# Second attention of a two-block transformer kernel: split queries and keys through memory, one 192-column score product for two short ones

## What is computed

```python
DILATED_BRANCHES = ((128, 1), (512, 4), (2048, 16))
def dilated_attention(q, k, v, rel_bias):
    for window, dil in DILATED_BRANCHES:
        o, l = dilated_window_branch(q, k, v, rel_bias, window, dil)
        ...
    w = jax.nn.softmax(jnp.stack(lses, axis=0), axis=0)
    return jnp.einsum('ibsh,ibshd->bshd', w.astype(q.dtype), jnp.stack(outs, axis=0))
...
q, k, v, zu, zv = jnp.split(z, ...)          # z = rms_norm_2(x) @ w_in, 8 heads of 64
attn = dilated_attention(q * 64 ** -0.5, k, v, rel_bias)
mix = jnp.concatenate([attn, sgu], axis=-1) @ w_out
```

## Time and profile before

| | |
|---|---|
| Times of 3 runs | 2572.89, 2575.97, 2576.0 us |
| Median | 2575.97 us |
| Span of the profiled execution (first to last instruction) | 2570.8 us |
| Busy: PE, weight loads, DVE, ACT, POOL | 2539.0, 2118.1, 1558.9, 1063.0, 1254.9 us |
| Granted PE clock | 0.998 of full speed |
| DMA | 372.39 MB, 41.8% of the 16 engines' span |

### The profile page before, as it was taken

One profiled execution on the slowest core, in us unless ns is written; L12 is line 12 of the kernel. 1 busy time (PEld: TensorE's weight loads), 2 busy tenths in 40 slices (PEclk: granted clock), 3 DMA queues, 4 the chain that ended last, 5 costly groups with the idle time before them and its releaser, 6 DMA issues. The chain is left out here.

```text
span 2570.8 us, 35208 instructions
## 1 busy us (share of the span) xinstructions
PE 2539.0 (99%) x12974; PEld 2118.1 (82%) x12974; DVE 1558.9 (61%) x2581; ACT 1063.0 (41%) x2107; POOL 1254.9 (49%) x1003
## 2 busy tenths in 40 slices
PE   8999999999999999999999999999999999999998
PEld 7888888777888888888888878998889888888886
DVE  6455444685437545444698751168656666587787
ACT  5332333684224332322444541169745323254443
POOL 4587675354526656555231774548545444200204
PEclk9999999999999999999999999999999999999999
DMA  6565655706551222221752345423143333364434
GB/s 218 203 237 207 237 218 193 266 18 202 192 180 66 82 82 88 77 82 66 294 185 96 117 154 189 106 67 85 51 134 116 115 106 117 136 232 146 173 105 157
DMA packets 162710, 372.39 MB, mean 145 GB/s; under 512 B 21538, under 2 KB 42658, under 8 KB 158882
## 3 DMA queue, kind: packets, MB, share of 16 engines
q1 hardware_dynamic: 162540, 370.15, 41.8%
HBM read 268.01 MB, written 101.83 MB: 144 GB/s over the span
## 5 line engine op out<-in xcount | busy, mean ns | idle before, releaser
L2421 POOL TENSOR_TENSOR WL<-WRAW,WH 128x512 fp32r<-128x512 f32 (+1 forms) x150 | 249.9, 1668 | 298.6 <-ACT WH L1101 298.6
L856 PE MATMUL PS<-HH,WL 128*128 128x512 f32 (+1 forms) x976 | 367.2, 376 | 1.1 <-DVE HS L2022 1.1
L859 PE MATMUL PS<-HH,WH 128*128 128x512 f32 (+1 forms) x976 | 366.1, 375 | 0.0
L858 PE MATMUL PS<-HL,WH 128*128 128x512 f32 (+1 forms) x976 | 366.1, 375 | 0.0
L1658 DVE TENSOR_TENSOR WL<-TS,WH 128x512 fp32r<-128x512 f32 x228 | 225.6, 994 | 169.7 <-ACT WH L1101 169.6
L920 PE MATMUL PS<-WH,DAL 128*128 128x512 f32 x756 | 294.4, 389 | 0.1
L921 PE MATMUL PS<-WL,DAH 128*128 128x512 f32 x756 | 294.1, 389 | 0.0
L922 PE MATMUL PS<-WH,DAH 128*128 128x512 f32 x756 | 294.1, 389 | 0.0
L2612 POOL TENSOR_TENSOR X<-X,DV 128x512 f32<-128x512 f32 x56 | 89.7, 1628 | 353.4 <-DVE DV L2085 270.8
L1101 ACT ACTIVATE WH<-TS 128x512 fp32r<-128x512 f32 x228 | 138.4, 621 | 179.8 <-POOL TS L2437 179.6
L856 PEld LDWEIGHTS PS<-HH,WL 128*128 128x128 f32 x976 | 183.7, 188 | 34.2 <-DVE HS L2022 1.3
(11 more groups left out here) (422 smaller groups left out, 6052.9 us busy)
## 6 DMA issues: line engine op xcount, KB each, us to landing
WRAW<-in_u_f SPq DMA_DIRECT2D x56, 512.0 KB, 3.8
WRAW<-in_u_in SPq DMA_DIRECT2D x54, 512.0 KB, 4.1
WRAW<-scr_t SPq DMA_DIRECT2D x52, 512.0 KB, 3.7
scr_h<-HS SPq DMA_DIRECT2D x96, 256.0 KB, 2.0
WRAW<-in_u_gu SPq DMA_DIRECT2D x44, 512.0 KB, 3.4
scr_t<-TTa SPq DMA_DIRECT2D x19, 1024.0 KB, 4.8
WRAW<-in_u_out SPq DMA_DIRECT2D x24, 512.0 KB, 3.6
scr_x<-X SPq DMA_DIRECT2D x24, 512.0 KB, 4.9
```

The costliest lines, as they stand in the source:

```text
L856: e.matmul(PS[:, b, 0:wd], wl[:, blk(kk)], op_moving(q, kk, c0, wd, 0), start=(kk == 0), stop=False)
L858: e.matmul(PS[:, b, 0:wd], wh[:, blk(kk)], op_moving(q, kk, c0, wd, 1), start=False, stop=False)
L859: mm = e.matmul(PS[:, b, 0:wd], wh[:, blk(kk)], op_moving(q, kk, c0, wd, 0), start=False, stop=(kk == 3))
L2421: e.tensor_tensor(lo, raw, hi.bitcast(F32), ALU.subtract).then_inc(*c.inc("w_lo_p", i))
```

## The change

1. The projection takes q and k tiles in turn (q of two heads, k of the same two), by another order of the weight's columns. Each tile is now split when it is drained: ACT writes the high part QKH, DVE the low part QKL from the same PSUM bank. Keys are laid out in groups of 192 columns, 128 strided ones and a copy of 64 near ones.
2. SP stores both parts to memory (32 DMAs, 10.5 MB) and loads each head back with the parts in the rows PE wants: two DMAs for the keys (64x1536), four for the queries (64x1024), 1.8 MB a head (14.7 MB in all). Heads 0 and 1 are loaded before the attention, head h + 2 after the last scores of head h, ahead of its bias table.
3. PE's four short score products of a step become two of 192 columns.
4. ACT's `keys_hi`, `queries_hi` and POOL's `keys_lo`, `queries_lo` are gone. `spread` goes from ACT to POOL, with two ARB buffers.
5. Head 0's keys no longer sit in a weight slot, so one more weight unit of the output projection is split before the attention (N_EARLY 3).

```diff
-            pairs = [(qs[:, blk(i % 4)], key_hi(h)[:, :]), (qs[:, blk(i % 4)], key_lo(h))]
-            w.wait_ge(*c.at("k_dn", (h, 1, 2)))
-            w.wait_ge(*c.at("q_dn", s // 4))
+            kk, col = K2[h % 2], 512 * hf + 128 * r
+            w.wait_ge(*c.at(f"hd_{h % 2}", h))
+            q2 = [q[:, col:col + 128] for q in Q2[h % 2]]
...
-                e.matmul(PS[:, b, 0:128], q_, keys(k_, 256 * r + 128 * (1 - hf), [[1, 128]]),
-                         start=(x == 0), stop=(x == m - 1))
-            for x, (q_, k_) in enumerate(pairs):
-                mm = e.matmul(PS[:, b, 128:192], q_, keys(k_, 112 if hf else 128, [[1, 16], [256, 4]]),
-                              start=(x == 0), stop=(x == m - 1))
+            keys = kk[:, KW * (1 - hf) + 192 * r:KW * (1 - hf) + 192 * r + 192]
+            for x in range(2):
+                mm = e.matmul(PS[:, b, 0:192], q2[x], keys, start=(x == 0), stop=(x == 1))
...
# ACT, the q2 tiles
+            for hi, ps in qk2_parts(QKH, j, half, PS[:, bk.at(key), :]):
+                part = e.activation(hi, ps, ACT.Copy, scale=1.0 if j % 2 else -0.125)
+            part.then_inc(*c.inc("qk2_h", n))
...
# DVE, the q2 tiles
+            w.wait_ge(*c.at("qk2_h", n))
+            qk2_place_free(w, n)
...
+                    part = e.tensor_tensor(lo, ps, hi.bitcast(F32), ALU.subtract)
...
# POOL
+        def spread(u):
+            w.wait_ge(*c.at("c_r", u))
+            if u >= 2:
+                w.wait_ge(*bk.full(("pv", u - 2)))
+            r = AR[:, 2 * u % 8:2 * u % 8 + 2]
+            e.tensor_copy(ARB[:, u % 2, :, :], bass.AP(r.tensor, r.offset, [r.ap[0], [1, 2], [0, 64]])).then_inc(
+                *c.inc("c_ra", u))
+            w.wait_ge(*c.at("c_ra", u))
...
+            if s % 2 == 0 and 0 <= u + 1 < N_EV:
+                spread(u + 1)
             if u >= 0 and s % 2 == 1:
                 values_lo(u)
...
# SP
+        def load_head(h):
+            p, j, rows = h % 2, h // 2, slice(64 * (h % 2), 64 * (h % 2) + 64)
+            for x, half in enumerate((slice(0, 64), slice(64, 128))):
+                e.dma_start(K2[p][half, :].bitcast(F32), scr_k2[x][j][rows, :]).then_inc(*c.inc(f"hd_{p}", (h, x), 16))
...
+                n = 2 * j + half
+                if n:
+                    store_qk2(n - 1)
...
                 if h + 2 < 8:
+                    w.wait_ge(*bk.full(("s2", s)))
+                    load_head(h + 2)
                     w.wait_ge(*bk.out(("s2", s)))
```

More of the change, by code:

```diff
@@ L31 @@
 NPAIR = 27
+KW = 768
 GAM = [1.0 - 2.0 ** (-5.0 - h) for h in range(4)]
@@ L215, in build @@
     P2 = at("P2", [P, 4, 768], 100 + 16)
[L216 to L219, removed]
     RBC = at("RBC", [P, P], MI + 26)
-    ARB = at("ARB", [P, 2, 64], 68 + 31.5)
+    ARB = at("ARB", [P, 2, 2, 64], B1 + 30)
     VR = [at("VRa", [P, 512], MI + 7.5), at("VRb", [P, 512], 68 + 29.5)]
@@ L1468, in act_program @@
         w.wait_ge(*c.at("b_w", 0))
-        for j in range(8):
-            key = "q2", j, 1
+        for n in range(16):
+            j, half = n // 2, n % 2
+            key = "q2", j, half
             w.wait_ge(*bk.full(key))
[L1472 to L1476, removed]
+            qk2_place_free(w, n)
+            for hi, ps in qk2_parts(QKH, j, half, PS[:, bk.at(key), :]):
+                part = e.activation(hi, ps, ACT.Copy, scale=1.0 if j % 2 else -0.125)
+            part.then_inc(*c.inc("qk2_h", n))
             feed(key)
@@ L1563, in beside @@
             h, i = A2[s]
-            if i % 4 == 0 and 2 <= s // 4 + 1 < n2 // 4:
-                queries_hi(s // 4 + 1)
-            if i in (1, 3) and h < 7:
-                keys_hi(h + 1, i // 2)
             if s in SPLIT_STEPS and ready(n_split[0], ("s2", s)):
@@ L2191, in dve_program @@
         w.wait_ge(*c.at("b_w", 0))
-        for j in range(8):
-            key = "q2", j, 0
-            w.wait_ge(*bk.full(key))
-            row = (Q2 if j < 4 else K2)[:, j % 4, :]
-            e.tensor_scalar(bass.AP(row.tensor, row.offset + (127 if j < 4 else 0),
-                                    [row.ap[0], [256, 4], [-1 if j < 4 else 1, 128]]),
-                            PS[:, bk.at(key), :].rearrange("p (l r) -> p r l", r=4), -0.125 if j < 4 else 1.0, None,
-                            ALU.mult).then_inc(*bk.free(key))
-            feed(("q2", j, 1))
+        for n in range(16):
+            j, half = n // 2, n % 2
+            key = "q2", j, half
+            w.wait_ge(*c.at("qk2_h", n))
+            qk2_place_free(w, n)
+            his = qk2_parts(QKH, j, half, PS[:, bk.at(key), :])
+            for (lo, ps), (hi, _) in zip(qk2_parts(QKL, j, half, PS[:, bk.at(key), :]), his):
+                if j % 2:
+                    part = e.tensor_tensor(lo, ps, hi.bitcast(F32), ALU.subtract)
+                else:
+                    part = e.scalar_tensor_tensor(out=lo, in0=ps, scalar=-0.125, in1=hi.bitcast(F32), op0=ALU.mult,
+                                                  op1=ALU.subtract)
+            part.then_inc(*bk.free(key))
+            if half:
+                feed(key)
         w.wait_ge(*c.at("gating", "all"))
@@ L2733, in pool_program @@
             if s < n2:
-                h, i = A2[s]
-                if i % 4 == 0 and 2 <= s // 4 + 1 < n2 // 4:
-                    queries_lo(s // 4 + 1)
-                if i in (1, 3) and h < 7:
-                    keys_lo(h + 1, i // 2)
                 if s in SPLIT_STEPS and ready(n_split[0], ("s2", s)):
@@ L3165, in sync_program @@
         w.wait_ge(*c.at("z_b", 7))
+        w.wait_ge(*c.at("ts0", ("out", 26)))
         load_g(0)
```

119 lines of the change are left out of this document (47 added, 72 removed).

## The result

The changed kernel takes 2578.63 us (median of 12 runs), the kernel before 2573.86 us in runs taken beside them: a ratio of 1.0019, interval 1.0011 to 1.0026. It is 4.8 us slower, where 3.1 us less was forecast. The profiled executions say the same on a smaller scale, 2573.9 us of span against 2570.8. The profiled execution of the changed kernel, 2575.69 us, is the second fastest of its 12 and 2.9 us under their median; that of the kernel before, 2572.89 us, is 1.0 under its median.

What follows compares the result with a forecast made beforehand. PE was taken as the bound, busy 2539.0 of 2570.8 us. Short products -8.0, step 24's wait -1.9 and new ARB waits +6.8 sum to -3.1 us, taking 2575.97 to 2572.9 us; range 2565.0 to 2578.5 us.

Steps and rivals of the forecast that it cites:

- Cost: nothing, between 0 and 2 us: Projection of q and k: extra drains, SP's 32 stores and one more POOL weight split never hold up PE.
- The short score products: PE's scores in the attention: two products instead of four save 0.125 us a step on average, 8.0 us over 64 steps.
- Where a new wait stands: POOL's ARB copy behind weight splits at s = 19, 23, 31, 39: PE waits 1.7 us four times, 6.8 us more.
- The wait of step 24: Attention, step 24: PE's wait for POOL's low part of the queries goes, 1.9 us less.
- The head's DMAs: Attention: 1.8 MB per head ahead of the bias table take 4.9 us, leaving 2.1 us of cover, so cost nothing.
- The second rival: Bias tables late at first use in heads 2 to 7: 12 us more, 2584.9 us in all; chance 0.1.
- The first: The rival that POOL makes the ARB copy in time or the four waits are hidden: -9.9 us, 2566.1 us; chance 0.25.
- the third rival: Short score products cost by columns only, so save nothing, and the four waits stand: +2.9 us, 2578.9 us; chance 0.05.

Runs made afterwards that it cites:

- e2: Changed kernel, but POOL makes the next even step's ARB copy before the weight split instead of after it; 2576.34 us, ratio 1.0006 to the kernel before.
- e3: Changed kernel, but each score product of 192 columns is again two, of 128 and 64 columns, layout kept; 2588.68 us, ratio 1.0054 to the kernel before.
- e4: Kernel of e2, but SP asks for a head's bias table before its queries and keys; 2600.49 us, ratio 1.0100 to the kernel before.
- e1: Changed kernel, but ACT instead of SP issues the 32 stores of split queries and keys; 2571.52 us, ratio 0.9991 to the kernel before.
- e5: Changed kernel with both edits, stores issued by ACT and ARB copy ahead of the weight split; 2567.76 us, ratio 0.9978 to the kernel before.
- e9: Kernel of e5, but queries and keys of heads 2 to 7 are not loaded; 2560.53 us, ratio 0.9945 to the kernel before.
- e11: Kernel of e5, but K2 and Q2 parts interleaved in neighbouring partitions, three transfers into 128 partitions per head; 2563.97 us, ratio 0.9960 to the kernel before.
- e10: Kernel of e5, but a head's six transfers become three into 128 partitions, parts outermost; 2751.31 us, ratio 1.0687 to the kernel before.

## Why the prediction was wrong

The forecast was -3.1 us, and +4.8 came (+3.1 in the spans). It also started from 2575.97 us, the median of three runs, where twelve give 2573.86; against those its 2572.9 was a gain of 1 us. By its own steps, on the spans:

- **The failed step: "Cost: nothing, between 0 and 2 us", for the projection.** It cost 7.7 us in the profiled execution, and more in those of e2, e3 and e4 (e1 takes all of it away). The text counted PSUM's eight banks as the cover and SP as "behind by a tile at most". But the new buffers QKH and QKL are only two deep, and each of their places comes free through SP's queue, in order, behind a wait for POOL's sums. The delay did not stay a tile: drain waits for store, store for sums, and it ran down the stage until the eight banks were used up. The stores, given less than 4.9 us, took 5.1 to 7.0 from issue to landing (medians of the four kinds). Of the 7.7 us the lower clock took 1.8.
- **"The short score products", -8.0.** They gave 0.19 us per step, -12.2, outside the bounds of 6.4 to 10.6 (e3). Mechanism right, size off. The first product had 0.10 and takes 0.08 to 0.09; the wider last one was given 0.26 us before L1018 and takes 0.20, no more than the narrow one's 0.21; and the step's other products follow 0.05 us per pair sooner.
- **"Where a new wait stands", +6.8.** Right in place, cause and number of splits: 1.2 to 2.25 us of idle time at three of the four places, 2.0 to 2.3 us more per pair where 1.7 was given. The chain back to ACT's weight split did not get shorter, while PE got there another 0.3 us earlier. At the fourth place the wait for the table stood in its stead; in e3, with slower steps, all four waits are for ARB.
- **The wait of step 24, -1.9.** Right.
- **"The head's DMAs", "Cost nothing".** Wrong by two choices. The table of head 5 was looked at, but that of head 3 has three weight units ahead of it. And 4.9 us for the 1.8 MB came from a busy stretch of another shape, at 375 GB/s; into 64 partitions they take 8.2 us of the engines (e5 against e9). The second rival had its threshold at 7 us of transfer per head, and that was passed. Its price was not 2.0 us at each of six heads, though: the tables of heads 5 to 7 still fit, and those of heads 3 and 4 cost about 3 of the 9.3 us of the long pairs, partly hidden behind the ARB waits.

A rule of the Trainium skill stood against this change and was not weighed: "SBUF — State Buffer", section "Door 1: The DMA port swizzle (why `[64,N]` ≈ `[32,N]`)". It says that a transfer into 64 partitions reaches half of the memory's ports and moves little more than one into 32, 196 GB/s where 128 partitions get 328. The trace agrees in kind: 246 against 392 to 416 GB/s, with transfers into both halves queued behind one another, and it adds that the engines show as full in both cases. By its 196 GB/s a head's 1.8 MB take 9.2 us, an estimate from the page, beyond the 7 us from which the second rival decides; that rival deserved more than a tenth.

The sum: +7.7 - 12.2 - 1.9 + 9.3 = +2.9, against +3.1 measured in the spans. So two large misses of opposite sign, +7.7 in the projection and -4.2 in the short products, partly hid each other; that the forecast came as near as it did is luck. The first and the third rival are out, the one because all four pairs were long, the other by the 0.19 us. (In the chances the third rival is called "the same" but added to "slower"; by its own words it is 0.56 to 0.10.)

## What to carry to other kernels

When a drain goes to a small buffer that is stored away, the cover is the depth of that buffer and not PSUM's, and the release runs through every wait ahead of the store in the issuing engine's queue; put the store on the queue of the engine that fills the buffer. Rate a new transfer by rows of the same shape (partitions, outermost dimension), and look at the place where most bytes stand ahead of it. Waits beside each other hide one another: mending the ARB waits alone (e2) shortened the attention by 1.2 us of the 9.3 of the long pairs, and mending the start alone (e1) made it 2.5 us longer.

## What the runs showed of the hardware

- **Half the partitions, over a third of the rate gone.** Transfers into 64 partitions held the DMA share at 1.03 with 246 GB/s (e5), the same data into 128 moved 392 GB/s at 0.99 (e11). With the same bytes in all, 143 GB/s over the attention, the mean share was 0.65 and 0.53.
- **The outermost dimension deals out the engines.** With 2 outermost, share 0.13 and 55 GB/s, and 178 us on the kernel. The Trainium skill has this in "DMA: Bandwidth & Descriptors", section "Rules for kernel authors": an outermost dimension below 16 confines a transfer to at most that many engines. The trace agrees, 0.13 being two of sixteen.
- **An issue takes longer where transfers are crowded or slow.** In the attention half of SP's issues took 0.6 us or less before and in e5; the longest took 3.0 us before, 5.3 in the crowded heads of e5, and in e10 13.35 us and more, and everything behind them in SP's program waited too.
- **PE's clock is part of the price of a stop.** Behind 4.8 us of idle time (e2) the granted clock was 0.50, 1.2 GHz, over the next 5 us. Short stops went either way: behind 1.6 us (e1) and 2.2 us (e11) it was 0.50 too, for 3 us, and the next pair took 2.0 us more; behind the waits of 1.2 to 2.25 us for ARB in the changed kernel it stayed at 1.00.
